# Attention on one core: where the output turns and the next tile's query parts stand in the eight-step schedule

## The chip, the cores and the metric

The kernel runs on one core of a Trainium2 chip. The metric is the device time of one launch in microseconds (us). Five engines run their own instruction streams and meet through semaphores: PE (TensorE, matrix multiplications; PEld are its weight loads), ACT (ScalarE), DVE (VectorE), POOL (GpSimd) and SP (SyncE, which issues the DMAs here).

## The reference

One layer of a diffusion backbone on 2048 latent tokens and 128 context tokens, D = 1024: a combined input projection, attention (8 query heads, 2 key/value heads, head size 64) beside a bidirectional retention, an output projection, a router and 16 expert networks. The part that the change touches is the attention:

```python
def block_attention(q, k, v):
    ...
    def one_block(qblk):
        s = jnp.einsum('bkgqd,bskd->bkgqs', qblk, k).astype(jnp.float32) * scale
        p = jax.nn.softmax(s, axis=-1).astype(v.dtype)
        return jnp.einsum('bkgqs,bskd->bkgqd', p, v)
    o = lax.map(one_block, qb)
    return o.transpose(1, 0, 4, 2, 3, 5).reshape(B, T, N_Q_HEADS * HEAD_DIM)
```

Latent queries read 2048 latent and 128 context keys, that is 17 key tiles of 128; context queries read the 128 context keys.

## The kernel before

The program runs stage after stage: input projection, retention, attention, output projection, selection of tokens for the experts, experts. In the trace the attention lies between about 608 and 1518 us.

**Tiles and steps.** The attention works through 17 tiles of 128 queries: 16 latent ones (`i` = 0 to 15) and the context tile (`i` = 16). Tiles 0, 1, 15 and 16 are straight code, 2 to 14 are a loop. A tile has eight steps, `h` = 0 to 7, one for each head. The order of the work within a step is written out by hand, once for each engine, in `PE_STEP`, `ACT_STEP` and `DVE_STEP` (L1109 to L1114). On PE a step is: turns 0 and 1 (`turn`, L1488: transposes of the head's probabilities, four 128x128 pieces to a bank), values 0 and 1 (`value`, L1508: probabilities times values, for the pair of heads before), turn 2, scores 2 (`scores`, L1478, two heads ahead), turn 3, scores 0, value 2, the fold place, turn 4 (one piece), scores 1.

**The fold place.** In even steps it holds `fold` (L1520: the two halves of a pair's output are added). In steps 5 and 7 it holds `mod` (L1531: two columns of the adaLN modulation). In steps 1 and 3 it is empty.

**The two turn banks.** All results of turns, folds, `mod`, query turns (`q`) and output turns (`out`) go by turns to the PSUM banks `ps_t[0]` and `ps_t[1]`, in PE's order. Each use raises `filled[b]`; whoever reads the bank last raises `emptied[b]`, and the use after next waits for it. A turn is first copied by ACT (`pT_hi`, L1620) and then read by DVE (`pT_lo`, L1712), which empties the bank. A fold is emptied by DVE (`combine`, L1755, which writes `att`), query turns and output turns by ACT.

**The output turns.** `turn_out` (L1534, transposes at L1542) turns the finished heads `att` of the tile before, two transposes for heads 0 to 3 (`out` 0) and two for heads 4 to 7 (`out` 1). Heads 4 to 7 are complete after the fold of step 2. Both stand behind everything else in step 3, and before the first of them PE waits until both banks have been emptied of all earlier uses:

```python
if half_at == 0:
    for b in range(2):
        pe.wait_ge(emptied[b], bank.uses_of(b))
```

ACT copies them to `attT` (L1628), SP stores `attT` (L1388).

**The next tile's queries.** SP loads the queries `q_row` of the next tile but one after `queries_lo` has freed the buffer. ACT makes their high parts (`queries_hi`, L1600) after step 4, DVE the low parts (`queries_lo`, L1677) ahead of everything in step 5. PE turns them (`turn_queries`, L1459) at the head of step 6.

**Other work.** ACT runs `exps` (L1609) and `keep_sums` (L1632), which takes a pair's value sums out of PSUM ahead of the turns of an even step and lets PE begin the next pair's `value` 0. DVE runs the maxima (`maxima`, L1685). POOL multiplies the modulation's weights.

Of the kernel before, what the change touches and what calls it, by code (L numbers as in the profile page):

```python
# [15 lines left out]
NQ = 8  # L16
# [1161 lines left out]
def attention(nc, g, a, s, marks, spent):  # L1178


    with ExitStack() as ctx:
# [11 lines left out]
        fold = k.sb("a_fold", [P, HD])  # L1193
# [26 lines left out]
        filled, emptied = k.sems("a_filled", 2), k.sems("a_emptied", 2)  # L1220
# [2 lines left out]
        wm_in, gain_ok, whole = k.sems("a_wm_in", 2), k.sem("a_gain_ok"), k.sem("a_whole")  # L1223
        m_step, ones_ok = k.sems("a_m_step", 2), k.sem("a_ones_ok")
        STEPS = 2 * DC - 1
        MOD_STEPS = (5, 7)
        LATE = EARLY + NT
        assert LATE == SCALE2 and 2 * LATE + NT == 2 * GATE2
        wmod_v = [a["w_mod"][0].rearrange("(k p) (e n) -> e p k n", p=P, n=w) for w in (P, HALF)]
# [13 lines left out]
        def segs_of(i):  # L1243
            return [2] if isinstance(i, int) and i == NT else SEG_ORDER
# [30 lines left out]
        def score_of(i, h):  # L1275

            return (i, h + 2) if h < NQ - 2 else (i + 1, h + 2 - NQ)

        def exp_of(i, h):
            return (i, h + 1) if h < NQ - 1 else (i + 1, 0)  # L1280

        def step_events(i, h, order=PE_STEP):

            last_tile = isinstance(i, int) and i == NT
            first_tile = isinstance(i, int) and i == 0
            folds = h % 2 == 0 and not (first_tile and h < 4)
            takes_part = {"scores": lambda n: not (last_tile and h >= NQ - 2) and n in segs_of(score_of(i, h)[0]),
                          "exp": lambda n: not (last_tile and h == NQ - 1) and n in segs_of(exp_of(i, h)[0]),
                          "turn": lambda n: n in turns_of(i), "total": lambda n: h % GROUP == GROUP - 1,
                          "mod": lambda n: True, "fold": lambda n: folds, "keep": lambda n: folds,  # L1290
                          "value": lambda n: not (first_tile and h < 2)}
            head = [("q", 0), ("q", 1)] if h == NQ - 2 and not last_tile else []
            tail = [("out", 0), ("out", 1)] if h == 3 and not first_tile else []
            if h in MOD_STEPS and not last_tile:
                order = [("mod", MOD_STEPS.index(h)) if kind == "fold" else (kind, n) for kind, n in order]
            return head + [(kind, n) for kind, n in order if takes_part[kind](n)] + tail

        def uses(i):
            return sum(e[0] in BANKED for h in range(NQ) for e in step_events(i, h))
# [41 lines left out]
        @block.sync  # L1341
        def _(sp):
            for c in range(DC):
                sp.dma_start(w_out[:, c, :], a["w_out"][0, c * P:(c + 1) * P, :]).then_inc(w_out_in, 16)
            for sem, stored in g["retained"]:
                sp.wait_ge(sem, stored)
            sp.sem_inc(stored_ok, 1)
            set_back(nc, spent)

            def load_mod(i, n):  # L1350

                e = (EARLY, 2 * LATE)[n] + i
                if not (isinstance(i, int) and i == 0):
                    sp.wait_ge(m_step[n], i * STEPS)
                sp.dma_start(wm[n][:, :, :], wmod_v[n][e] if isinstance(e, int) else
                             wmod_v[n][bass.ds(e, 1)].rearrange("a p k n -> (a p) k n")).then_inc(wm_in[n], 16)

            def body(i):
                if isinstance(i, int) and i == NT:
                    sp.wait_ge(att_out, 16 * (NT - 1))  # L1360
                    for n in range(2):
                        sp.dma_start(g["heads"][n][:, :, :].rearrange("p c t -> p (c t)"), s["ct"][n]).then_inc(g["heads_in"][n], 16)
                    sp.dma_start(g["router"][:, :, :], a["w_router"][0].rearrange("(c p) e -> p c e", p=P)).then_inc(g["router_in"], 16)
                else:
                    for n in range(2):
                        load_mod(i, n)
                    sp.wait_ge(q_lo_ok, i + 1)
                    src = s["q"][i + 1] if isinstance(i, int) else s["q"][bass.ds(i + 1, 1)].rearrange("a p n -> (a p) n")
                    sp.dma_start(q_row[:, :, :].rearrange("p h f -> p (h f)"), src).then_inc(q_in, 16)
                bank = Bank(i)  # L1370
                for h in range(NQ):
                    for kind, n in step_events(i, h):
                        if kind in BANKED:
                            b, before = bank.next()
                            if kind == "out":
                                sp.wait_ge(emptied[b], before + 1)
                            if kind == "out" and n == 1:
                                store(i - 1)
                if isinstance(i, int) and i == NT:
                    bank.next(), bank.next()  # L1380
                    for half_at in range(2):
                        b, before = bank.next()
                        sp.wait_ge(emptied[b], before + 1)
                    store(NT)

            def store(t):
                dst = s["ct"][t] if isinstance(t, int) else s["ct"][bass.ds(t, 1)].rearrange("a p n -> (a p) n")
                sp.dma_start(dst[:, 0:4 * P], attT[:, :, :].rearrange("p c t -> p (c t)")).then_inc(att_out, 16)  # L1388

            tiles(sp, body)  # L1390
            g["attended"] = (att_out, 16 * NTA)

# [45 lines left out]
        def _(pe):  # L1438
# [94 lines left out]

            def turn_out(t, half_at, bank):  # L1534

                if half_at == 0:
                    for b in range(2):
                        pe.wait_ge(emptied[b], bank.uses_of(b))
                b, before = bank.next()
                for n in range(2):  # L1540
                    c = 2 * half_at + n
                    ins = nc.tensor.transpose(ps_t[b][:, n, :], att[:, 2 * c:2 * c + 2, :].rearrange("p h f -> p (h f)"),  # L1542
                                              g["ident"][:, :])
                ins.then_inc(filled[b], 1)
# [44 lines left out]
        def _(act):  # L1589
# [53 lines left out]
            def body(i):  # L1643
                last_tile = isinstance(i, int) and i == NT
                bank = Bank(i)
                for h in range(NQ):
                    bank_of = bank.step(i, h)
                    for kind, n in step_events(i, h, ACT_STEP):
                        if kind == "exp":
                            exps(*exp_of(i, h), n)  # L1650
                        elif kind == "keep":
                            keep_sums(*fold_of(i, h))
                        else:
                            leave(i, h, kind, n, *bank_of[kind, n])
                    if h == NQ - 4 and not last_tile:
                        queries_hi(i + 1)
                if last_tile:
                    keep_sums(i, NGRP - 2)
                    b, before = bank.next()
                    act.wait_ge(filled[b], before + 1)  # L1660
                    keep_sums(i, NGRP - 1)
                    bank.next()
                    for half_at in range(2):
                        leave(i + 1, 0, "out", half_at, *bank.next())

            tiles(act, body)

        @block.vector
        def _(dve):
# [5 lines left out]
            def queries_lo(i):  # L1675
                dve.wait_ge(q_hi_ok, i + 1)
                nc.vector.scalar_tensor_tensor(out=q_parts[:, :, 1, :], in0=q_row[:, :, :], scalar=-SCALE,  # L1677
                                               in1=q_parts[:, :, 0, :].bitcast(F32), op0=ALU.mult, op1=ALU.subtract)\
                    .then_inc(q_lo_ok, 1)
# [80 lines left out]
            def body(i):  # L1760
                last_tile = isinstance(i, int) and i == NT
                bank = Bank(i)
                for h in range(NQ):
                    if h == NQ - 3 and not last_tile:
                        queries_lo(i + 1)
                    bank_of = bank.step(i, h)
                    for kind, n in step_events(i, h, DVE_STEP):
                        if kind == "scores":
                            maxima(*score_of(i, h), n)
                        elif kind == "total":  # L1770
                            total(i, h)
                        elif kind == "mod":
                            keep_modulation(i, n, *bank_of[kind, n])
                        else:
                            leave(i, h, kind, n, *bank_of[kind, n])
                if last_tile:
                    for grp in (NGRP - 2, NGRP - 1):
                        combine(i, grp, *bank.next())
# [1301 lines left out]
```

## Time and profile before

| | |
|---|---|
| median of 3 runs | 3103.34 us (3103.21 to 3105.35) |
| the profiled execution, its own time | 3105.5 us |
| its span | 3103.8 us |
| mean granted TensorE clock over the span | 0.973 of full speed |
| PE busy over the span | 2945.4 us (95%) |
| DVE, ACT, POOL busy | 1832.8, 1665.6, 701.7 us |

The span is what the trace covers; the time of an execution lies 1.7 us above it. The busy shares are means over stages with different limits, so the attention is read from rows of its own.

### The profile page before, as it was taken

What the parts mean: (1) busy time and instruction counts of PE and PEld (TensorE: products, weight loads), DVE (VectorE), ACT (ScalarE), POOL (GpSimd) and SP (SyncE); (2) the same over time, 40 slices, a digit from 0 to 9 for tenths busy, and PEclk for the clock granted to TensorE, in tenths of its full rate; (3) what the DMA queues carried; (4) which work ended last, traced back from release to release, by engine and by line L of the source; (5) the groups of instructions that cost most, each with busy time, mean ns of one, the idle gap of its engine ahead of it and who ended that gap; (6) DMA issues with size and microseconds to landing.
All of it is one profiled execution on the core that took longest, in us unless ns stands there. A gap on an engine that the chain in (4) does not pass through costs nothing. (4 is left out here: it accounts for less than half of the span.)

```text
span 3103.8 us, 57542 instructions
## 1 busy us (share of the span) xinstructions
PE 2945.4 (95%) x20880; PEld 2739.2 (88%) x20880; DVE 1832.8 (59%) x2989; ACT 1665.6 (54%) x3227; POOL 701.7 (23%) x878
## 2 busy tenths in 40 slices
PE   8999997899999999999899869999999999999996
PEld 5888886788988888888788769999999999999996
DVE  6222225788888888888533386655555555555555
ACT  4222223677878777787443426554444544444544
POOL 1333334642323232232000011111111111111104
PEclk9999998999999999999899869999999999999998
DMA  7211116411010010101164425566666666666657
GB/s 259 85 68 68 68 61 195 179 26 35 17 30 20 17 34 17 34 17 35 61 217 143 142 95 181 186 197 192 191 191 193 197 197 194 194 194 197 195 181 283
DMA packets 320129, 394.75 MB, mean 127 GB/s; under 512 B 30260, under 2 KB 276488, under 8 KB 319016
## 3 DMA queue, kind: packets, MB, share of 16 engines
q1 hardware_dynamic: 307416, 356.18, 34.5%
q0 software_dynamic: 12240, 36.77, 4.8%
q8 instruction: 55, 0.90, 0.1%
q10 hardware_dynamic: 384, 0.62, 0.1%
q14 instruction: 34, 0.28, 0.0%
HBM read 319.60 MB, written 74.06 MB: 127 GB/s over the span
## 5 line engine op out<-in xcount | busy, mean ns | idle before, releaser
L2880 DVE TENSOR_TENSOR e_w_lo<-e_raw,e_w_hi 128x2048 fp32r<-128x2048 f32 x189 | 433.3, 2292 | 411.9 <-ACT e_w_hi L2797 411.9
L94 PE MATMUL e_ps<-e_x_hi,e_w_hi 128*128 128x272 f32 x2048 | 602.5, 294 | 3.0 <-issue 3.0
L96 PE MATMUL e_ps<-e_x_hi,e_w_lo 128*128 128x272 f32 x2048 | 594.3, 290 | 0.0
L95 PE MATMUL e_ps<-e_x_lo,e_w_hi 128*128 128x272 f32 x2048 | 590.7, 288 | 0.0
L1620 ACT ACTIVATE a_pT_hi<-a_ps_t 128x512 fp32r<-128x512 f32 (+1 forms) x648 | 327.0, 531 | 150.0 <-PE a_ps_t L1488 149.2
L1685 DVE TENSOR_REDUCE a_mx<-a_ps_s 128x1 f32<-128x896 f32 (+2 forms) x392 | 351.8, 898 | 87.6 <-PE a_ps_s L1478 79.1
L1712 DVE TENSOR_TENSOR a_pT_lo<-a_ps_t,a_pT_hi 128x512 fp32r<-128x512 f32 (+1 forms) x648 | 367.6, 600 | 40.0 <-ACT a_pT_hi L1620 39.3
L94 PEld LDWEIGHTS e_ps<-e_x_hi,e_w_hi 128*128 128x128 f32 x2048 | 387.1, 189 | 3.2 <-issue 3.2
L95 PEld LDWEIGHTS e_ps<-e_x_lo,e_w_hi 128*128 128x128 f32 x2048 | 388.0, 189 | 0.0
L96 PEld LDWEIGHTS e_ps<-e_x_hi,e_w_lo 128*128 128x128 f32 x2048 | 386.4, 189 | 0.0
L1478 PE MATMUL a_ps_s<-a_keys,a_qT 128*128 128x448 f32 (+2 forms) x1296 | 352.8, 386 | 14.2 <-ACT a_prob L1609 13.4
L2797 ACT ACTIVATE e_w_hi<-e_raw 128x2048 fp32r<-128x2048 f32 x189 | 360.6, 1908 | 0.0
L1488 PE MATMUL a_ps_t<-ident,a_prob 128*128 128x128 f32 x2184 | 333.4, 277 | 19.1 <-DVE a_pT_lo L1712 8.8
L1609 ACT ACTIVATE a_prob<-a_ps_s,a_nm 128x896 f32<-128x896 f32 (+2 forms) x392 | 332.6, 857 | 2.5 <-DVE a_nm L1693 2.5
L1488 PEld LDWEIGHTS a_ps_t<-ident,a_prob 128*128 128x128 f32 x2184 | 255.2, 143 | 56.6 <-DVE a_pT_lo L1712 16.8
L94 PE MATMUL e_ps<-e_h_hi,e_w_hi 128*128 128x272 f32 x1024 | 298.9, 292 | 0.8 <-DVE e_h_lo L2965 0.8
L96 PE MATMUL e_ps<-e_h_hi,e_w_lo 128*128 128x272 f32 x1024 | 296.9, 290 | 0.0
L95 PE MATMUL e_ps<-e_h_lo,e_w_hi 128*128 128x272 f32 x1024 | 295.1, 288 | 0.0
L1508 PE MATMUL a_ps_o<-a_pT_hi,a_vals 128*128 128x256 f32 x1092 | 280.9, 292 | 3.0 <-DVE a_pT_lo L1712 2.2
L1508 PE MATMUL a_ps_o<-a_pT_lo,a_vals 128*128 128x256 f32 x1092 | 269.2, 281 | 0.0
L94 PE MATMUL p_psP<-p_w_hi,p_hhi 128*128 128x512 f32 (+1 forms) x680 | 252.3, 371 | 5.8 <-DVE p_hlo L477 2.8
L95 PE MATMUL p_psP<-p_w_lo,p_hhi 128*128 128x512 f32 (+1 forms) x680 | 251.0, 369 | 0.0
(357 smaller groups left out, 5459.9 us busy)
## 6 DMA issues: line engine op xcount, KB each, us to landing
e_raw<-in_w_gate SPq DMA_DIRECT2D x64, 1024.0 KB, 4.8
e_raw<-in_w_up SPq DMA_DIRECT2D x64, 1024.0 KB, 4.8
e_raw<-in_w_down SPq DMA_DIRECT2D x64, 1024.0 KB, 5.0
s_ret<-p_pr SPq DMA_DIRECT2D x17, 768.0 KB, 3.6
p_raw<-in_w_in SPq DMA_DIRECT2D x8, 1152.0 KB, 17.8
o_cT<-s_ct SPq DMA_DIRECT2D x17, 512.0 KB, 4.9
s_x<-o_x SPq DMA_DIRECT2D x17, 512.0 KB, 5.0
s_xn<-o_xn SPq DMA_DIRECT2D x17, 512.0 KB, 3.5
```

Of the source, the lines that this page charges most:

```text
L94: nc.tensor.matmul(out, w_hi, x_hi, start=first, stop=False)
L95: nc.tensor.matmul(out, w_hi, x_lo, start=False, stop=False)
L96: return nc.tensor.matmul(out, w_lo, x_hi, start=False, stop=last)
L1478: ins = nc.tensor.matmul(ps_s[:, b, 0:w], qT[:, h, :], keys[:, part, h // QPK, src:src + w], start=(part == 0), stop=(part == 1))
L1488: ins = nc.tensor.transpose(ps_t[b][:, c % 4, :], prob[h % 2][:, c * P:(c + 1) * P], g["ident"][:, :])
L1508: ins = nc.tensor.matmul(ps_o[:, :, :], vals[:, src, grp * GROUP // QPK, :, :].rearrange("p d f -> p (d f)"), part[grp % 2][:, c, :, :], s ...
L1609: nc.scalar.activation(seg_probs(i, h, seg), seg_scores(seg, seg_width(i, seg)), ACT.Exp, bias=nm[:, h % 2:h % 2 + 1], scale=-1.0, accum_o ...
L1620: nc.scalar.activation(out, ps_t[b][:, 0:out.shape[1], :], ACT.Copy).then_inc(hi_kept, 1)
L1685: nc.vector.tensor_reduce(mx[:, h % 2, seg:seg + 1], seg_scores(seg, seg_width(i, seg)), AXY, ALU.min)\
L1712: nc.vector.tensor_tensor(pT_lo[h // 2 % 2][:, out, h % 2, :], ps_t[b][:, 0:m, :], pT_hi[h // 2 % 2][:, out, h % 2, :].bitcast(F32), ALU.s ...
L2797: nc.scalar.activation(w_hi[n % RING][:, :, :], raw[n % RING][:, :, :], ACT.Copy).then_inc(w_hi_ok, 1)
L2880: nc.vector.tensor_tensor(w_lo[n % RING][:, :, :], raw[n % RING][:, :, :], w_hi[n % RING][:, :, :].bitcast(F32), ALU.subtract).then_inc(w_ ...
```

## The change

The two output turns leave the end of step 3. `out` 0 goes to the fold place of step 1 and `out` 1 to that of step 3, on PE between value 2 and turn 4, on ACT between `exps` 1 and the copy of turn 4. PE's wait for both banks is replaced by the wait that every other use has, for the use before the last. SP waits only for the second output turn. `queries_hi` goes from the end of step 4 to the end of step 3 on ACT, `queries_lo` from the head of step 5 to behind turn 1 of step 4 on DVE. The number of uses of the banks in a tile stays the same; in steps 2 and 3 the banks change places.

```diff
-        MOD_STEPS = (5, 7)
+        MOD_STEPS, OUT_STEPS = (5, 7), (1, 3)
...
             head = [("q", 0), ("q", 1)] if h == NQ - 2 and not last_tile else []
-            tail = [("out", 0), ("out", 1)] if h == 3 and not first_tile else []
             if h in MOD_STEPS and not last_tile:
                 order = [("mod", MOD_STEPS.index(h)) if kind == "fold" else (kind, n) for kind, n in order]
-            return head + [(kind, n) for kind, n in order if takes_part[kind](n)] + tail
+            if h in OUT_STEPS and not first_tile:
+                slot = [j for j, e in enumerate(order) if e in (("fold", 0), ("turn", 4))]
+                order = order[:slot[0]] + [("out", OUT_STEPS.index(h))] + order[slot[0]:]
+            return head + [(kind, n) for kind, n in order if takes_part[kind](n)]
...
-                            if kind == "out":
+                            if kind == "out" and n == 1:
                                 sp.wait_ge(emptied[b], before + 1)
-                            if kind == "out" and n == 1:
                                 store(i - 1)
...
             def turn_out(t, half_at, bank):
-                if half_at == 0:
-                    for b in range(2):
-                        pe.wait_ge(emptied[b], bank.uses_of(b))
                 b, before = bank.next()
+                pe.wait_ge(emptied[b], before)
...
-                    if h == NQ - 4 and not last_tile:
+                    if h == NQ - 5 and not last_tile:
                         queries_hi(i + 1)
...
-                    if h == NQ - 3 and not last_tile:
-                        queries_lo(i + 1)
                     bank_of = bank.step(i, h)
                     for kind, n in step_events(i, h, DVE_STEP):
...
+                        if (h, kind, n) == (NQ - 4, "turn", 1) and not last_tile:
+                            queries_lo(i + 1)
```

## Rows read from the trace of the kernel before

**Rows 1.** Windows in the attention: length, busy us (instructions) of each engine, clock, DMA

```profile
1040.00:1100.00 60.00, 58.00 (x428) 53.30 (x427) 51.78 (x99) 47.25 (x107) 17.66 (x33) 1.00 0.09 26
...
1500.00:1520.00 20.00, 11.28 (x46) 8.55 (x44) 7.08 (x31) 7.65 (x25) 0.10 (x1) 0.55 0.11 33
```

**Rows 2.** Waits from 700 to 1460 us: who for whom, us in total, times, longest

```profile
PE a_ps_s L1478 <- ACT a_prob L1609: 7.7, 28, 0.3
...
PE a_ps_t L1488 <- DVE a_pT_lo L1712: 5.9, 14, 0.6
...
PE a_ps_t L1488 <- ACT a_attT L1628: 4.6, 14, 0.3
```

**Rows 3.** Timeline of PE: start, length, instructions; steps 1 to 7, context tile last

```profile
1066.13 1.04 PE L1488 MATMUL a_ps_t<-ident,a_prob 128*128 128x128 f32 x8
...
1071.00 0.27 PE L1488 MATMUL a_ps_t<-ident,a_prob 128*128 128x128 f32 x1
1071.54 1.08 PE L1478 MATMUL a_ps_s<-a_keys,a_qT 128*128 128x448 f32 x4 [0.27 <-ACT a_prob L1609]
1072.46 1.04 PE L1488 MATMUL a_ps_t<-ident,a_prob 128*128 128x128 f32 x8
...
1078.83 1.06 PE L1488 MATMUL a_ps_t<-ident,a_prob 128*128 128x128 f32 x8
...
1083.66 0.27 PE L1488 MATMUL a_ps_t<-ident,a_prob 128*128 128x128 f32 x1
1084.20 1.08 PE L1478 MATMUL a_ps_s<-a_keys,a_qT 128*128 128x448 f32 x4 [0.27 <-ACT a_prob L1609]
1085.27 0.63 PE L1542 MATMUL a_ps_t<-ident,a_att 128*128 128x128 f32 x4
1086.23 1.09 PE L1488 MATMUL a_ps_t<-ident,a_prob 128*128 128x128 f32 x8 [0.34 <-ACT a_attT L1628]
...
1092.62 1.09 PE L1488 MATMUL a_ps_t<-ident,a_prob 128*128 128x128 f32 x8
...
1095.49 0.66 PE L1488 MATMUL a_ps_t<-ident,a_prob 128*128 128x128 f32 x4 [0.41 <-DVE a_pT_lo L1712]
...
1099.53 1.04 PE L1459 MATMUL a_ps_t<-ident,a_q_parts 128*128 128x128 f32 x8
...
1107.30 1.09 PE L1488 MATMUL a_ps_t<-ident,a_prob 128*128 128x128 f32 x8
...
1113.65 1.09 PE L1488 MATMUL a_ps_t<-ident,a_prob 128*128 128x128 f32 x8
...
1502.55 1.09 PE L1542 MATMUL a_ps_t<-ident,a_att 128*128 128x128 f32 x4 [0.78 <-DVE a_pT_lo L1712]
```

**Rows 4.** Timeline of ACT: turn 0 of step 2, then steps 3 and 4

```profile
1073.10 1.09 ACT L1620 ACTIVATE a_pT_hi<-a_ps_t 128x512 fp32r<-128x512 f32 x2 [1.17 <-PE a_ps_t L1488]
...
1083.06 1.00 ACT L1609 ACTIVATE a_prob<-a_ps_s,a_nm 128x896 f32<-128x896 f32 x1
...
1084.04 0.28 ACT L1620 ACTIVATE a_pT_hi<-a_ps_t 128x128 fp32r<-128x128 f32 x1
1085.80 0.66 ACT L1628 ACTIVATE a_attT<-a_ps_t 128x256 f32<-128x256 f32 x2 [1.48 <-PE a_ps_t L1542]
1086.34 0.39 ACT L1632 ACTIVATE a_o_sum<-a_ps_o 128x256 f32<-128x256 f32 x1
...
1092.15 0.62 ACT L1600 ACTIVATE a_q_parts<-a_q_row 128x512 fp32r<-128x512 f32 x1
```

**Rows 5.** Timeline of DVE: step 2, step 3, head of step 5

```profile
1075.75 0.56 DVE L1685 TENSOR_REDUCE a_mx<-a_ps_s 128x1 f32<-128x384 f32 x1 [0.56 <-PE a_ps_s L1478]
...
1082.64 1.29 DVE L1712 TENSOR_TENSOR a_pT_lo<-a_ps_t,a_pT_hi 128x512 fp32r<-128x512 f32 x2
...
1094.14 0.69 DVE L1677 SCALAR_TENSOR_TENSOR a_q_parts<-a_q_row,a_q_parts 128x512 fp32r<-128x512 f32 x1
1094.75 1.28 DVE L1712 TENSOR_TENSOR a_pT_lo<-a_ps_t,a_pT_hi 128x512 fp32r<-128x512 f32 x2
```

More of the change, by code:

```diff
@@ L1289, in step_events @@
                           "turn": lambda n: n in turns_of(i), "total": lambda n: h % GROUP == GROUP - 1,
-                          "mod": lambda n: True, "fold": lambda n: folds, "keep": lambda n: folds,
+                          "mod": lambda n: True, "out": lambda n: True, "fold": lambda n: folds, "keep": lambda n: folds,
                           "value": lambda n: not (first_tile and h < 2)}
             head = [("q", 0), ("q", 1)] if h == NQ - 2 and not last_tile else []
-            tail = [("out", 0), ("out", 1)] if h == 3 and not first_tile else []
             if h in MOD_STEPS and not last_tile:
                 order = [("mod", MOD_STEPS.index(h)) if kind == "fold" else (kind, n) for kind, n in order]
-            return head + [(kind, n) for kind, n in order if takes_part[kind](n)] + tail
+            if h in OUT_STEPS and not first_tile:
+                slot = [j for j, e in enumerate(order) if e in (("fold", 0), ("turn", 4))]
+                order = order[:slot[0]] + [("out", OUT_STEPS.index(h))] + order[slot[0]:]
+            return head + [(kind, n) for kind, n in order if takes_part[kind](n)]
         def uses(i):
```

## The prediction

> **What bounds the kernel now.** I read first the windows over the attention, because the change touches nothing else: PE is busy 58.00 of 60 us there at a granted clock of 1.00, that is 2.4 GHz, while DVE has 51.78, ACT 47.25 and POOL 17.66 us [rows 1]. PE is the bound of this stage, so only what PE waits for is worth anything, and an engine beside it costs only where it makes PE wait. The second view is the list of waits over 14 tiles: PE's own idle time ends at three places in each tile: twice (28 times) at scores 1, for ACT's exponentials, once (14 times) at a turn, for DVE's low parts, and once at the turn behind the output turns, for ACT's `attT` copy [rows 2]. These entries add to 18.2 us in 14 tiles, but that understates the loss: PE's lengths are modelled, and a wait also holds up issue where the row shows no idle time. So the third view is PE's timeline, read from the start of one step's turn 0 to the next one's [rows 3]:
>
> - step 1: 1066.13 to 1072.46, 6.33 us; step 2: to 1078.83, 6.37;
> - step 3: to 1086.23, 7.40; step 4: to 1092.62, 6.39;
> - step 5: to the query turns at 1099.53, 6.91; step 7: 1107.30 to 1113.65, 6.35.
>
> Two steps stand out. Step 3 is 1.07 us longer than step 1, which does the same work but has no output turns. Step 5 is 0.56 longer than step 7, which also has a `mod` in the fold place; its turn 2 waits until 1095.49 for DVE's low part of turn 0, and that is late because `queries_lo` ran at 1094.14 ahead of it [rows 3, 5]. These are the steps of one loop tile; the counts of 14 in the waits say that the others have the same two waits.
>
> **The output turns leave the end of step 3.** What goes is the whole difference: the wait for both banks, four transposes (0.63 us), and the wait until ACT has emptied them, 1.07 us for each of the latent tiles 1 to 15, 15 x 1.07 = 16.0 us.
>
> What they cost in the fold places of steps 1 and 3 is bounded by what is idle there. In both, turn 4 starts at 1071.00 or 1083.66 and scores 1 only 0.54 later, at 1071.54 or 1084.20, since scores 1 waits for ACT's last exponential (1083.06 + 1.00 = 1084.06) [rows 3, 4]. The 0.54 us hold one transpose now and would hold three. Four in the end of step 3 take 0.63, so two add at most 0.32; with the one of turn 4 (0.27) that is 0.59, 0.05 too long. Below it: four transposes of a turn issue closer together than their row lasts, so nothing at all may be added. Step 7 is the nearest step with work in that place, and it is 0.02 longer than step 1. I take 0.02: 30 places x 0.02 = 0.6 us. The upper end is three transposes at the 0.27 of a single one, 0.81 - 0.54 = 0.27 each, 8.1 us.
>
> The Trainium skill (TensorE: Matmul & The Clock Gate, Part 4: PE-mode transpose) gives about 275 ns for a 128x128 transpose in a kernel; paid whole, three would need 0.83 us, an estimate from that page, and the sum below would shrink by about 8.6 us. The trace agrees for a single one (0.27), but not for a row of them, four in 0.63 [rows 3].
>
> The change puts a different bank wait into these steps. With six uses instead of five, `out` waits for turn 2's bank and turn 4 for turn 3's. DVE does turns 2 and 3 from 1082.64 to 1083.93, so turn 2's bank is free at about 1083.3, before `out` would start at 1083.66, and turn 3's at 1083.93, 0.27 us ahead of the 1084.20 at which scores 1 can start [rows 3, 5]. One transpose fits into that; if DVE were later by more than about 0.15 us, the excess would fall on PE.
>
> On ACT the copy of two transposes takes 0.33 (0.66 for both) and stands ahead of turn 4's copy. Queued behind it are that copy, DVE's low part of turn 4, and at the end `keep_sums` of the next step. ACT had waited 1.17 us before the next step's first copy (1073.10) and 1.48 before the output copies (1085.80) [rows 4]; this idle time hides the copy. If it were gone, 0.33 per place would be paid. SP's single wait stands for both output turns, since ACT works in order; the store and the weight loads behind it on SP are issued about two microseconds earlier, into DMA queues at 0.09 of their capacity [rows 1].
>
> **High parts of the queries one step sooner.** 0.62 us on ACT [rows 4] move ahead of `keep_sums` of step 4, for which PE's value 0 waits. This is the dangerous edit, so I lay the instants end to end. Without the tail, step 4 starts where step 2 does relative to scores 1, 0.92 behind it (1071.54 to 1072.46), at 1085.12. ACT: the output copy can start when its transposes are through, as at the tail 0.53 behind their start (1085.27 to 1085.80), at 1084.19; turn 4's copy at 1084.5; high parts from about 1084.7 to 1085.3; `keep_sums` (0.39) until 1085.7. Turn 0's copy is possible 0.64 behind its transposes (1072.46 to 1073.10), at 1085.76; ACT is just free. Value 0 follows turns 0 and 1 (1.04 to 1.09 long), at about 1086.0. Slack 0.3, so I take 0; the other end, the whole 0.62 on PE in 16 tiles, would be 9.9 us. SP issues the load right behind the low parts of the tile before, most of a tile earlier, so `q_in` holds nothing up.
>
> **Low parts half a step sooner.** From step 5 goes 0.56 us in each of the tiles 0 to 15: 16 x 0.56 = 9.0 us. In step 4 the 0.61 us of `queries_lo` (1094.14 to 1094.75) stand between turn 1 and the maximum of scores 2, where DVE idled 0.56 for PE in step 2 [rows 5]. 0.05 remain, and I count them on PE: 16 x 0.05 = 0.8 us. Lower end 0, since DVE has more slack further on; upper end the whole 0.61, 9.8 us. Behind it wait turns 2 to 4 and the maxima of step 4, and for these PE's fold and turn 4. SP's next query load, which waits for `queries_lo`, comes sooner and is needed a tile later.
>
> **The context tile.** Here PE is not full: 11.28 of 20 us at a granted clock of 0.55, mostly the lower level of 1.2 GHz [rows 1]. Its output turns wait 0.78 and take 1.09 [rows 3]. Between 0 and 1.9 us go; I take 1.0.
>
> **Sum.** 16.0 + 9.0 + 1.0 - 0.6 - 0.8 = 24.6 us saved. Against the profiled execution (3105.5 us, span 3103.8) that is 3080.9; it lay 2.2 above the median, so the median of 3103.3 becomes 3078.7. The stages behind take over the shift whole: each begins with the results of the one before.
>
> **Rivals.** A difference of 0.2%, 6.2 us, is about what a measurement of this kernel can tell from no change.
>
> - *A, as summed*: 3078.7, own range 3074 to 3083, the ends of the small terms and some us for the clock at the stage's end. 0.70.
> - *B, the fold place is too narrow*: each of three transposes costs 0.27, or DVE's turn 3 is late by that much. 8.1 us come back: 3086. For it: 0.27 us of room by the rows, and two engines that must be in time at once. Against it: step 7. The page's 275 ns (above) would bring the same. 0.10.
> - *C, low parts not hidden in step 4*: DVE gives 9.8 back: 3088. For it: idle time and instruction are the same size to 0.05. Against it: one wait is 0.61 late only if no slack follows in the step. 0.10.
> - *D, no change*: the tail moves to another wait. With step 3 shortened, the first turns of step 4 would wait for DVE's low part of turn 4, which the removed wait covered. Steps 1 and 2 have the same neighbours and show no such wait, so 0.04; 3100 to 3106.
> - *E, slower*: `keep_sums` of step 4 behind the high parts holds value 0. Its slack is 0.3; it eats the gain of 1.6 us a tile when it is 1.9 late, and slower by 0.2% needs 2.3 us, some 3110. Only a late `q_in` could do that, since ACT's own work there (0.33, 0.28, 0.62 and 0.39) is 1.6 us in all. 0.03.
>
> The remaining 0.03 are for a time below 3074. Hence faster 0.93, same 0.04, slower 0.03. The range takes in A, most of B and C's end: 3074 to 3088.
>
> **What the changed profile would show.** Step 3 at 6.3 to 6.4 us from turn 0 to turn 0 and no wait of turns for `attT`; step 5 at about 6.35 to the query turns and turn 2 without a wait for DVE; step 4 up to 0.05 longer than 6.39; a loop tile shorter by 1.6 us, from query turns to query turns. B would show scores 1 of steps 1 and 3 starting more than 0.54 after value 2; C a wait for DVE's low parts or maxima in steps 4 and 5; E value 0 of step 4 waiting for `a_o_sum`. If the tile is shortened but the time isn't, a later stage sets the end and the sum was made in the wrong place.

## The result and the profile after

The changed kernel takes 3079.4 us (median of 4 runs, 3076.0 to 3081.9) beside 3104.4 us (median of 4 runs) of the kernel before: a ratio of 0.9919, 95% interval 0.9906 to 0.9931, or 25.0 us less. Forecast were 24.6 us less and 3078.7 us.

The stages after the attention have nearly the same length in both traces: from the output projection's first matrix multiplication (1521.21 us before, 1495.88 after) to the end of the span it is 1582.6 and 1582.0 us. All of the gain was made by then. PE's timeline of one loop tile, steps 1 to 5 of the changed kernel (start, length, instructions), answers to [rows 3]:

```profile
1056.21 1.04 PE L1489 MATMUL a_ps_t<-ident,a_prob 128*128 128x128 f32 x8
...
1061.07 0.38 PE L1541 MATMUL a_ps_t<-ident,a_att 128*128 128x128 f32 x2
1061.38 0.33 PE L1489 MATMUL a_ps_t<-ident,a_prob 128*128 128x128 f32 x1
1061.63 1.09 PE L1479 MATMUL a_ps_s<-a_keys,a_qT 128*128 128x448 f32 x4
1062.56 1.03 PE L1489 MATMUL a_ps_t<-ident,a_prob 128*128 128x128 f32 x8
...
1068.93 1.06 PE L1489 MATMUL a_ps_t<-ident,a_prob 128*128 128x128 f32 x8
...
1073.76 0.38 PE L1541 MATMUL a_ps_t<-ident,a_att 128*128 128x128 f32 x2
...
1075.22 1.03 PE L1489 MATMUL a_ps_t<-ident,a_prob 128*128 128x128 f32 x8
1076.01 0.36 PE L1509 MATMUL a_ps_o<-a_pT_hi,a_vals 128*128 128x256 f32 x1
...
1081.55 1.09 PE L1489 MATMUL a_ps_t<-ident,a_prob 128*128 128x128 f32 x8
1083.90 0.60 PE L1489 MATMUL a_ps_t<-ident,a_prob 128*128 128x128 f32 x4
...
1087.89 1.03 PE L1460 MATMUL a_ps_t<-ident,a_q_parts 128*128 128x128 f32 x8
```

From turn 0 to turn 0, step 3 takes 1068.93 to 1075.22, 6.29 us in place of 7.40. Step 5, from its turn 0 to the query turns, takes 1081.55 to 1087.89, 6.34 in place of 6.91; its turn 2 starts 2.35 behind turn 0, without a wait, where it stood 2.87 behind. The output turns stand in what was idle time: scores 1 of step 1 starts 0.56 behind the start of the output turn, as it started 0.54 behind that of turn 4. PE's waits in the loop tiles (who for whom, us in total, times, longest), from 700 to 1430 us, answer to [rows 2]:

```profile
PEld a_ps_t L1489 <- ACT a_qT L1622: 6.8, 14, 0.5
PEld a_ps_t L1489 <- DVE a_att L1754: 6.7, 30, 0.2
PEld a_ps_t L1489 <- DVE a_pT_lo L1711: 6.5, 30, 0.3
PEld a_ps_t L1489 <- issue: 5.6, 26, 0.2
PE a_ps_t L1489 <- ACT a_qT L1622: 3.5, 14, 0.3
```

None of the three PE waits in [rows 2] is listed any more. Two of them have gone; the third, scores 1 for ACT's exponential, is still there, but work now fills it (e5). What is listed for PE is its wait for ACT's copy of the query turns, 0.25 us a tile. It isn't new: the list of the kernel before has it too, beside the three that the prediction named:

```profile
PE a_ps_t L1488 <- ACT a_qT L1623: 3.5, 14, 0.3
```

### The profile page after: what moved, and what is told of

It reads as the page before. It is cut to its first block and busy times, and to the rows that moved or that the text cites. A ratio compares the mean times of both kernels' runs of the same rounds, so it can differ in the third digit from the quotient of the medians.

```text
span 3077.9 us, 57496 instructions
## 1 busy us (share of the span) xinstructions
PE 2943.4 (96%) x20880; PEld 2742.6 (89%) x20880; DVE 1831.1 (59%) x2989; ACT 1664.6 (54%) x3227; POOL 700.9 (23%) x878
## 5 line engine op out<-in xcount | busy, mean ns | idle before, releaser
L96 PE MATMUL p_psP<-p_w_hi,p_hlo 128*128 128x512 f32 (+1 forms) x680 | 251.2, 369 | 0.0
```

What stands on the lines that cost most here:

```text
L96: return nc.tensor.matmul(out, w_lo, x_hi, start=False, stop=last)
```

## The experiments

Each kernel ran against the kernel before on one chip, e8 and e10 on another chip than the rest; "us" is the median. The steps are those of one loop tile near 1060 us, from turn 0 to the next turn 0, step 5 to the start of the query turns or, where these have left the head of step 6, to its turn 0. From tile to tile they differ by some 0.05.

| kernel | us | ratio to before (95%) | step 1 | 2 | 3 | 4 | 5 |
|---|---|---|---|---|---|---|---|
| before | 3104.4 to 3105.3 | | 6.33 | 6.37 | 7.40 | 6.39 | 6.91 |
| changed | 3079.4 | 0.9919 (0.9906 to 0.9931) | 6.35 | 6.37 | 6.29 | 6.33 | 6.34 |
| e1, output turns only | 3083.2 | 0.9936 (0.9919 to 0.9952) | 6.34 | 6.36 | 6.30 | 6.33 | 6.92 |
| e2, queries only | 3098.5 | 0.9981 (0.9972 to 0.9991) | 6.34 | 6.37 | 7.40 | 6.67 | 6.29 |
| e3, output turns and high parts | 3084.1 | 0.9935 (0.9918 to 0.9951) | 6.34 | 6.33 | 6.33 | 6.33 | 6.91 |
| e4, low parts twice | 3086.0 | 0.9944 (0.9927 to 0.9960) | 6.34 | 6.32 | 6.34 | 6.96 | 6.32 |
| e5, output turns twice | 3078.8 | 0.9913 (0.9896 to 0.9931) | 6.32 | 6.33 | 6.35 | 6.33 | 6.34 |
| e6, end with single wait | 3101.8 | 0.9988 (0.9979 to 0.9998) | 6.33 | 6.36 | 7.25 | 6.39 | 6.90 |
| e7, output turns at ends | 3095.5 | 0.9972 (0.9961 to 0.9984) | 6.55 | 6.72 | 6.50 | 7.01 | 6.28 |
| e8, high parts only | 3107.4 | 1.0009 (1.0000 to 1.0018) | 6.34 | 6.36 | 7.42 | 6.67 | 6.95 |
| e9, packed | 3067.0 | 0.9880 (0.9862 to 0.9898) | 6.79 | 6.36 | 6.68 | 6.33 | 6.34 |
| e10, packed further | 3058.3 | 0.9854 (0.9839 to 0.9869) | 6.59 | 6.38 | 6.29 | 6.40 | 6.26 |

My theory was that of the prediction: two gains apart from each other, the end of step 3 and DVE's late turn in step 5, and every moved instruction hidden in idle time of its engine. Rivals: one chain, in which step 5 is late only because step 4 is; a fold place too narrow; query parts that are not hidden.

**e1, the output turns alone.** The changed kernel with `queries_hi` and `queries_lo` back in their places.

```diff
-                    if h == NQ - 5 and not last_tile:
+                    if h == NQ - 4 and not last_tile:
                         queries_hi(i + 1)
...
+                    if h == NQ - 3 and not last_tile:
+                        queries_lo(i + 1)
...
-                        if (h, kind, n) == (NQ - 4, "turn", 1) and not last_tile:
-                            queries_lo(i + 1)
```

> The output turns go to the fold places of steps 1 and 3, both query parts stay where the kernel before has them. Theory of two separate gains: step 3 falls from 7.40 to about 6.3 us, step 5 keeps its 6.91 with the wait of turn 2 for DVE; 15 tiles x 1.1 and 1.5 us of the context tile, 17 to 18 us faster than the kernel before, about 3087. Rival, one chain: the wait in step 5 is an after-effect of the late step 4 (ACT and DVE start it late behind the output copies), so it shrinks with the end of step 3; then step 5 comes to 6.6 or less and the kernel to about 3080 to 3082.

Step 3 falls to 6.30 and step 5 stays at 6.92. The rival of one chain falls. The time is 21 us below that of before, some 3 better than I expected; step by step, 15 tiles x (1.10 + 0.06) and the context tile's 1.7 (below) make 19. Step 4 became 0.06 shorter (6.33) with the query parts in their old places, so that gain too belongs to the output turns.

**e2, the queries alone**, in the kernel before: the same lines the other way round.

> High and low parts go to their new places, the output turns stay at the end of step 3. Two separate gains: step 5 falls from 6.91 to 6.35, step 3 keeps 7.40; 16 x 0.56 = 9 us faster than before, about 3095. One chain: little or nothing of step 5 is gained while the end of step 3 is as it was, 3100 or more. A second rival, that the high parts ahead of the pair's sums in step 4 hold up value 0: step 4 longer than 6.39 by up to 0.6, and the kernel not faster than before.

The second rival is right here, in part. Step 5 falls to 6.29, but step 4 grows to 6.67: 0.34 us net a tile, and the time falls by 5.9 us. ACT's timeline of steps 3 and 4 in this kernel:

```profile
1086.04 0.66 ACT L1628 ACTIVATE a_attT<-a_ps_t 128x256 f32<-128x256 f32 x2 [1.48 <-PE a_ps_t L1542]
1086.58 0.63 ACT L1600 ACTIVATE a_q_parts<-a_q_row 128x512 fp32r<-128x512 f32 x1
1087.10 0.38 ACT L1632 ACTIVATE a_o_sum<-a_ps_o 128x256 f32<-128x256 f32 x1
```

and PE's:

```profile
1086.47 1.09 PE L1488 MATMUL a_ps_t<-ident,a_prob 128*128 128x128 f32 x8 [0.34 <-ACT a_attT L1628]
...
1087.54 0.39 PE L1508 MATMUL a_ps_o<-a_pT_hi,a_vals 128*128 128x256 f32 x1
```

The pair's sums end at 1087.48 and value 0 starts at 1087.54, 1.07 behind turn 0, where a step without this wait has it at 0.79 (1093.14 to 1093.93 in the same trace).

**e8, the high parts alone**, in the kernel before: `queries_hi` to the end of step 3, nothing else. It asks which of the two query parts lengthened step 4 in e2.

> The kernel before with one edit: the high parts go to the end of step 3, behind the output copies that still stand there; low parts at the head of step 5. In the run with both query parts moved, step 4 grew by 0.25 us. If the high parts did that (ACT is late with the pair's sums, and value 0 waits), step 4 is 6.6 to 6.7 here too, with a wait of the values for the sums, and the time is level with before or up to 4 us above it. If the low parts on DVE did it, step 4 keeps 6.39 and the time that of before.

Step 4 is 6.67 again, and the values wait for the sums (2.5 us in 12 tiles); the high parts did it. The time is level with that of before to 0.2% slower.

**e3, output turns and high parts**, low parts in their old place (the changed kernel with the second and third part of e1's diff).

> The output turns in the fold places and the high parts after step 3; the low parts stay at the head of step 5. If the high parts on ACT ahead of the pair's sums are hidden (slack of 0.3 us by my instants), step 4 is 6.3 to 6.4 and the time is that of the run with the output turns alone, within 1 us. If they are not hidden, step 4 is longer and the time up to 10 us above that run's.

Step 4 is 6.33, the time that of e1 to within 1 us. Once the output copies have left the end of step 3, the high parts cost nothing there. ACT's timeline in the changed kernel answers to [rows 4]:

```profile
1074.18 0.39 ACT L1627 ACTIVATE a_attT<-a_ps_t 128x256 f32<-128x256 f32 x1
1074.46 0.27 ACT L1619 ACTIVATE a_pT_hi<-a_ps_t 128x128 fp32r<-128x128 f32 x1
1074.63 0.62 ACT L1599 ACTIVATE a_q_parts<-a_q_row 128x512 fp32r<-128x512 f32 x1
1075.15 0.37 ACT L1631 ACTIVATE a_o_sum<-a_ps_o 128x256 f32<-128x256 f32 x1
1075.85 1.09 ACT L1619 ACTIVATE a_pT_hi<-a_ps_t 128x512 fp32r<-128x512 f32 x2 [0.33 <-PE a_ps_t L1489]
```

The sums end at 1075.52, 0.30 behind turn 0 of step 4 (1075.22), and ACT still idles 0.33 before the copy of turn 0.

**e4, the low parts twice.** The changed kernel; DVE executes the instruction of the low parts twice in step 4 (the new semaphore `q_once` sets the second behind the first) and writes the same values twice.

```diff
             def queries_lo(i):
                 dve.wait_ge(q_hi_ok, i + 1)
+                nc.vector.scalar_tensor_tensor(out=q_parts[:, :, 1, :], in0=q_row[:, :, :], scalar=-SCALE,
+                                               in1=q_parts[:, :, 0, :].bitcast(F32), op0=ALU.mult, op1=ALU.subtract)\
+                    .then_inc(q_once, 1)
+                dve.wait_ge(q_once, i)
                 nc.vector.scalar_tensor_tensor(out=q_parts[:, :, 1, :], in0=q_row[:, :, :], scalar=-SCALE,
```

> The changed kernel, with the instruction of the low parts executed twice in a row in step 4 (the same values written twice). The prediction said that DVE's idle time there (0.56 us) just holds one (0.61). If that idle time is all the cover, the second costs its 0.6 to 0.7 us in step 4 or 5 of each of 16 tiles: 10 us slower than the changed kernel, about 3089. If DVE has more slack further on in the step before PE needs it, less than half of that: under 3084.

DVE's timeline of step 4, first in the changed kernel, then with two:

```profile
1076.65 1.29 DVE L1711 TENSOR_TENSOR a_pT_lo<-a_ps_t,a_pT_hi 128x512 fp32r<-128x512 f32 x2
1077.86 0.68 DVE L1676 SCALAR_TENSOR_TENSOR a_q_parts<-a_q_row,a_q_parts 128x512 fp32r<-128x512 f32 x1
1078.45 0.55 DVE L1684 TENSOR_REDUCE a_mx<-a_ps_s 128x1 f32<-128x384 f32 x1
```

```profile
1079.07 0.68 DVE L1676 SCALAR_TENSOR_TENSOR a_q_parts<-a_q_row,a_q_parts 128x512 fp32r<-128x512 f32 x1
1079.78 0.69 DVE L1680 SCALAR_TENSOR_TENSOR a_q_parts<-a_q_row,a_q_parts 128x512 fp32r<-128x512 f32 x1
1080.39 0.55 DVE L1688 TENSOR_REDUCE a_mx<-a_ps_s 128x1 f32<-128x384 f32 x1
```

The first instruction costs step 4 nothing (6.33 as in e1, where it isn't there); the second, which starts 0.71 behind the first, costs 0.63 (6.96), and PE's fold waits for DVE (2.7 us in 13 waits). By the steps 16 tiles lose 10 us, as expected; the median, 3086.0, lies only 6.6 above the changed kernel's, which was timed on its own, and lies between the two forecasts. The cover holds one instruction and less than 0.1 us more, little above the 0.56 of idle time read from [rows 5].

**e5, the output turns twice.** The changed kernel with four transposes in each of the two places (each output piece turned twice).

```diff
-                for n in range(2):
+                for n in (0, 1, 0, 1):
                     c = 2 * half_at + n
                     ins = nc.tensor.transpose(ps_t[b][:, n, :], att...
```

> The changed kernel with each output transpose done twice, so that four stand in each place of steps 1 and 3 (the same result written twice). It asks how much room the 0.54 us between turn 4 and scores 1 has. If transposes issue closer than their rows last (four in 0.35 us), two more add about 0.18 to a place that has little left: steps 1 and 3 go from 6.33 to 6.4 or 6.5, 2 to 5 us slower than the changed kernel, 3081 to 3084. Rival, each paid whole at 0.27: five transposes are 1.35, steps 1 and 3 grow by 0.5 each, 15 us slower, about 3094.

Neither: it costs nothing in a loop tile. PE's timeline of step 1, then ACT's:

```profile
1057.41 0.60 PE L1541 MATMUL a_ps_t<-ident,a_att 128*128 128x128 f32 x4
1057.85 0.27 PE L1489 MATMUL a_ps_t<-ident,a_prob 128*128 128x128 f32 x1
1057.96 1.08 PE L1479 MATMUL a_ps_s<-a_keys,a_qT 128*128 128x448 f32 x4
```

```profile
1056.82 1.00 ACT L1608 ACTIVATE a_prob<-a_ps_s,a_nm 128x896 f32<-128x896 f32 x1
```

The exponential ends at 1057.82 and scores 1 starts 0.14 later, as in the kernel before (1084.06 to 1084.20). Five transposes take 0.55 from the first one's start to the start of scores 1, one every 0.11 us, and fill the place without lengthening it.

**e6, the end of step 3 with the single wait**, in the kernel before.

```diff
-                if half_at == 0:
-                    for b in range(2):
-                        pe.wait_ge(emptied[b], bank.uses_of(b))
                 b, before = bank.next()
+                pe.wait_ge(emptied[b], before)
```

> The kernel before, output turns at the end of step 3 and query parts in their old places, but the wait for both banks replaced by the wait for the bank's use before the last. It divides the 1.07 us of the end of step 3. If the wait for both banks is only a part of it (scores 1 start to output turns 1.07 instead of the 0.92 that another step needs), 0.1 to 0.2 us a tile go: 2 to 3 us faster than before, about 3101. If the wait is most of it, step 3 falls to 6.6 or less: 3092 or less, and the new place would matter little.

Step 3 falls by 0.15, to 7.25. The wait for both banks was a seventh of the 1.07 us; the other 0.92 go with the place, that is, with the transposes and the wait until ACT has emptied the bank.

**e7, the output turns at the ends of steps 1 and 3.** The changed kernel, one output turn behind scores 1 of each.

```diff
-                slot = [j for j, e in enumerate(order) if e in (("fold", 0), ("turn", 4))]
-                order = order[:slot[0]] + [("out", OUT_STEPS.index(h))] + order[slot[0]:]
+                order = order + [("out", OUT_STEPS.index(h))]
```

> The changed kernel with the output turns at the ends of steps 1 and 3, behind scores 1, one in each, with single waits; query parts in the new places. It asks whether the place counts or only the division in two and the wait. If the place counts, each end costs its two transposes and the wait of the next turn 0 for a bank until ACT has copied it, 0.2 to 0.5 us a step: 6 to 15 us slower than the changed kernel, 3085 to 3094. If only the division and the wait count, it is within 2 us of the changed kernel.

16 us slower than the changed kernel, a little more than I gave it. Steps 1 and 3 take 0.2 more; steps 2 and 4 0.35 and 0.68, because now ACT's output copy, and in step 4 the high parts too, stand ahead of the pair's sums when PE wants them (values for the sums: 4.8 us in 13 waits). So the place counts; the division into two and the single wait, at the ends of the steps, bring nothing: steps 1 to 5 add to 33.06, as they do with the queries alone (e2, 33.07).

**e9, packed.** The places in odd steps seem to have room, and the list of waits after names the query turns' copy. The two modulation uses join the output turns in steps 1 and 3 (in tile 0 they stay in 5 and 7), and the two query turns go from the head of step 6 to the fold places of steps 5 and 7. ACT's high parts wait two steps longer, because the second query turn now reads the parts as late as step 7.

```diff
-            head = [("q", 0), ("q", 1)] if h == NQ - 2 and not last_tile else []
...
+            if h in Q_STEPS and not last_tile:
+                at = order.index(("turn", 4))
+                order = order[:at] + [("q", Q_STEPS.index(h))] + order[at:]
...
-                    act.wait_ge(scored[2], (i - 1) * NQ + 1)
+                    act.wait_ge(scored[2], (i - 1) * NQ + 3)
```

> A version that goes on from the changed kernel: the two modulation uses join the output turns in steps 1 and 3 (in tile 0 they stay in 5 and 7), and the two query turns leave the head of step 6 for the fold places of steps 5 and 7. If a place in an odd step hides about 0.45 us of PE, step 6 falls by the 1.3 us of the query turns and the wait for their copies, and steps 1, 3, 5 and 7 grow by 0.1 to 0.2 each: 0.6 to 1.0 us a tile, 10 to 16 us faster than the changed kernel, 3064 to 3070. If ACT's copy of four transposes (0.6) ahead of turn 4's copy holds up the next step, steps 5 and 7 grow by 0.5 or more and the time stays within 5 us of the changed kernel or above it.

3067.0, as hoped, though not by the sizes expected. Steps 5 and 7 take 6.34 each with a query turn in them, and step 6 falls from 7.77, query turns included, to 6.41. But steps 1 and 3 grow to 6.79 and 6.68, 0.46 and 0.35 above a step with an empty place (6.33). The steps of 15 tiles give some 8 of the 12 us; the rest is not accounted for here. PE's timeline of step 3 (behind value 2), and two waits over all loop tiles:

```profile
1067.36 0.38 PE L1544 MATMUL a_ps_t<-ident,a_att 128*128 128x128 f32 x2
1067.68 0.39 PE L1535 MATMUL a_ps_t<-a_ones,a_m_sum 128*64 128x1 f32 x4
1068.21 0.33 PE L1492 MATMUL a_ps_t<-ident,a_prob 128*128 128x128 f32 x1
```

```profile
PEld a_ps_t L1492 <- ACT a_attT L1630: 2.9, 14, 0.2
PEld a_ps_t L1535 <- DVE a_pT_lo L1714: 2.6, 13, 0.2
```

With two uses ahead of it, turn 4 needs the bank of the output turn and waits 0.2 us for ACT's copy; `mod`, now the second use, waits 0.2 for DVE to empty the bank of turn 3. Together that is the size of step 3's growth. Both stand in step 3 alone; step 1 grew more, and there the list names no bank's reader, so its growth is not explained.

**e10, packed further.** All four output transposes share one bank in step 3, both modulation results one bank in step 1; so no place has more than one use beside turn 4.

```diff
-            mod_steps = (5, 7) if first_tile else (1, 3)
+            mod_steps = (5,) if first_tile else (1,)
...
-        OUT_STEPS, Q_STEPS = (1, 3), (5, 7)
+        OUT_STEPS, Q_STEPS = (3,), (5, 7)
```

> The packed version goes one step on: all four output transposes in one bank use in step 3, both modulation results in one bank use in step 1, one query turn each in steps 5 and 7. In the packed version steps 1 and 3 grew by 0.46 and 0.35, with a wait of turn 4 for the output copy. If that wait (three uses in a place, so that turn 4 needs the first one's bank) is the cause, step 3 falls to 6.35, as four transposes alone took no time in their place, and step 1 to 6.4 to 6.7: 0.5 us a tile, 6 to 9 us faster than the packed version, 3058 to 3061. If the matrix work itself overfills the places, steps 1 and 3 together stay 0.6 or more above 12.7 and the time within 3 us of the packed version.

Step 3 is 6.29, step 1 6.59, the time 3058.3: 1.5% below the kernel before, and the wait for `attT` is gone. The wait of `mod` has gone with it. The two places together hold the same matrix products as in e9, so it wasn't their work alone that had made steps 1 and 3 longer by the 0.59 that they now lose; the edit also makes one copy on ACT of two, which no run tells apart. Step 1 now holds eight small products (0.82 us), more than its place:

```profile
1049.40 0.82 PE L1536 MATMUL a_ps_t<-a_ones,a_m_sum 128*128 128x1 f32 x8
1050.15 0.33 PE L1491 MATMUL a_ps_t<-ident,a_prob 128*128 128x128 f32 x1
1050.23 1.06 PE L1481 MATMUL a_ps_s<-a_keys,a_qT 128*128 128x448 f32 x4
```

## Why the prediction was right

*What bounds the kernel.* Right: PE sets the pace of the stage, and the stages behind took over the shift whole, to 0.6 us. The list of PE's waits was read short: it had a fourth place in each tile, the copy of the query turns. The change left that one alone, so the sum didn't need it; e9 went on from there.

*The end of step 3, 1.07 us a tile.* Measured 1.06 to 1.11. Its parts: 0.15 was the wait for both banks (e6). Beside it step 4 became 0.06 shorter (e1), which the prediction had put at nothing.

*The fold places, taken at 0.02 each.* Measured 0 to 0.02; the upper end (0.27, rival B) falls with e5, where even five transposes fit. What the place holds is set by ACT's exponential, and a row of transposes passes at 0.11 us each, not at the 0.27 that one lasts in the timeline. The trace of the kernel before had this price already: when PE turns the keys at the start of the stage, each row of two starts 0.22 behind the one before:

```profile
615.80 0.38 PE L1448 MATMUL a_ps_t<-ident,a_k_hi 128*128 128x128 f32 x2
616.02 0.38 PE L1448 MATMUL a_ps_t<-ident,a_k_lo 128*128 128x128 f32 x2
```

By it three transposes take 0.33 and fit into the 0.54, and neither the 0.59 nor the upper end was needed. The about 275 ns that the Trainium skill (TensorE: Matmul & The Clock Gate, Part 4: PE-mode transpose) gives, for bf16, agree with a single fp32 one here (0.27) and not with a row of them.

*The high parts, taken at 0.* Right by e3: the sums end at 1075.52, 0.49 ahead of value 0 (1076.01), where a slack of 0.3 was reckoned. But it hangs on the other edit: the same move in the kernel before costs 0.28 us in step 4 (e8), by the mechanism of rival E, and far less than the 1.9 us of lateness at which E was to eat the gain. The sum priced the two edits as independent, and got the right total because it laid the instants of step 4 with the output turns already gone.

*The low parts: 0.56 gained in step 5, 0.05 paid in step 4.* Step 5 gained 0.57. The 0.05 weren't paid: step 4 is 6.33 with the low parts in it and without them (e1, e3). With the 0.06 by which the output turns shortened step 4, its place in the sum was off by 0.11 us a tile, 1.8 us in all. That the cover just holds one instruction was right (e4): of a second one nearly all is paid, 0.63, as rival C has it.

*The context tile, taken at 1.0 from 0 to 1.9.* From the last query turns to the first matrix multiplication of the output projection it is 42.72 us before (1478.49 to 1521.21) and 41.03 after (1454.85 to 1495.88): 1.7 gained. But that is no better known than to 1.6: the same stretch took 42.73 and 41.11 in e2 and e8, whose context tile is that of the kernel before, and 39.43, 39.43 and 39.90 in e1, e3 and e4, whose context tile is the changed one.

*The sum.* A loop tile is 1.72 us shorter (query turns to query turns 54.22 before, 52.50 after), where the terms gave 1.07 + 0.56 - 0.04 - 0.05 = 1.54. From its first query turns to the output projection the attention lost 27.0 us (912.9 to 885.9), and 28.0 if tile 0 had run alike in both traces (last section). That is 3.4 more than forecast, 2.7 of it in 15 tiles and 0.7 in the context tile. The spans of the two traces differ by 25.9: the execution traced after began its attention 1.6 us later (609.94 in place of 608.31) and was 0.6 shorter behind it. In all the traces here that begin lies between 606.5 and 611.4, behind stages that no edit touches. The medians differ by 25.0. So the closeness of the total, 25.0 to 24.6, is in part luck, some 3 us of it, by differences between executions; the terms themselves are right to within that.

## What to carry to other kernels

Measure a step from the same instruction to the same instruction of a like step; the difference of two like steps gave 1.07 and 0.56 us, where the waits listed for them gave 0.34 and 0.41. A hole in the bound engine that a wait for another engine makes is free room, up to that engine's release. With two banks in turn, one use in it was free here, and with two the next one waited 0.2 us for the first one's reader (e9). Price a row of short instructions by the distance of their starts and not by the length of one: 0.11 us and not 0.27 for a transpose here. Before an instruction is moved ahead of another on a side engine, lay the instants end to end with all the edits in place, since one edit can be what makes room for another.

## What the runs showed of the hardware

The same first tile ran at different clocks. Windows from 608 us, of the kernel before and then of the changed one (length, busy of PE, PEld, DVE, ACT, POOL, then the granted clock):

```profile
608.00:630.00 22.00, 17.84 (x108) 15.74 (x108) 10.52 (x16) 12.31 (x22) 13.22 (x16) 0.85 0.71 251
630.00:667.00 37.00, 33.65 (x236) 30.22 (x237) 33.41 (x62) 29.10 (x67) 12.41 (x26) 1.00 0.11 30
```

```profile
608.00:630.00 22.00, 17.05 (x102) 14.91 (x101) 10.62 (x14) 11.97 (x21) 11.76 (x14) 0.81 0.72 251
630.00:667.00 37.00, 33.87 (x230) 29.86 (x229) 32.88 (x61) 29.09 (x66) 12.61 (x25) 0.96 0.11 30
```

Shorter windows of the same two executions show where they part, first of the kernel before, then of the changed one:

```profile
613.00:614.00 1.00, 1.00 (x6) 1.00 (x5) 0.14 (x1) 0.60 (x1) 1.00 (x2) 0.50 1.00 406
615.00:616.00 1.00, 1.00 (x11) 1.00 (x10) 0.44 (x1) 0.78 (x2) 1.00 (x1) 1.00 1.02 414
629.00:633.00 4.00, 2.76 (x20) 2.08 (x17) 3.43 (x7) 3.94 (x9) 3.61 (x6) 1.00 0.00 0
```

```profile
614.00:615.00 1.00, 1.00 (x6) 1.00 (x5) 0.48 (x1) 0.36 (x1) 1.00 (x1) 0.50 1.04 422
616.00:617.00 1.00, 1.00 (x12) 1.00 (x10) 0.26 (x2) 0.96 (x2) 1.00 (x1) 1.00 1.01 414
629.00:633.00 4.00, 3.44 (x15) 2.81 (x16) 3.22 (x5) 1.44 (x3) 3.61 (x6) 0.57 0.00 0
```

In both, the granted clock rose from 0.50 (1.2 GHz) to 1.00 (2.4 GHz) between the first two windows, while PE did nothing but transposes, those of the first queries and of the keys. In the kernel before it stayed there; in the changed kernel it was back at 1.2 GHz for most of 629 to 633 us (0.57). Shortly before, until 626.88, PE had waited 2.27 us for ACT's exponentials; but the other execution has the same wait (2.25 us) and no fall, so the traces don't show what decides. The steps up to the head of step 5 of tile 0, where the two programs do the same work but for the moved query parts, took 51.3 us (608.31 to 659.63) and 52.4 (609.94 to 662.29). That is 1.0 us of the difference between two executions, as large as the small terms of the sum.
